# Which engine adds the squared tiles: four tiles per retention head and per state-space group, on VectorE instead of GpSimd

## The chip, the cores and the metric

The kernel runs on one core of one Trainium2 chip. The metric is the device time of one execution in microseconds; several executions are timed and their median is compared. Besides, one execution was recorded by the hardware profiler, and all rows below come from it. PE is TensorE (PEld its weight loads), DVE is VectorE, ACT is ScalarE, POOL is GpSimd and SP is SyncE, which here only issues DMAs.

## The reference

The kernel computes a small network of three layers on 256 tokens of 1024 channels, in fp32. Two parts matter here.

The retention mixer has four heads. For each, `ret` (512 channels) is normalised over its own channels and multiplied with a gate:

```python
ret = (intra + cross.swapaxes(0, 1)).reshape(bsz, seq, B_HEADS, B_DV)
ret = rms_norm(ret, out_g.reshape(B_HEADS, B_DV)).reshape(bsz, seq, dv)
y = ret * jax.nn.silu(g.astype(jnp.float32))
```

The state-space mixer has four groups of 512 channels, and normalises each in the same way after the gate:

```python
y = y.reshape(b, seq, D_INNER).astype(h.dtype) * jax.nn.silu(z)
y = rmsnorm(y.reshape(b, seq, SSD_GROUPS, D_INNER // SSD_GROUPS),
            ssd_norm_w.reshape(SSD_GROUPS, D_INNER // SSD_GROUPS))
```

Each such norm needs, per token, the sum of the squares of 512 channels.

## The kernel before

Channels lie on the 128 partitions and tokens along the free axis, so 512 channels are four tiles of 128x256. All weights come from one stream of 381 slabs (128x1024 fp32, 512 KB each) through a ring of six buffers. SP loads a slab once DVE has finished with its buffer; ACT copies it, rounded, into `w_hi` (L177); DVE writes the rest into `w_lo` (L182, "the split"); PE multiplies each of eight blocks three times (L190 to L192). ACT is four slabs ahead of the one being multiplied, DVE three.

The sum of squares goes over three engines. ACT squares four tiles into `sq`. POOL adds tiles 2 and 3 onto 0 and 1 (128x512, L258), then tile 1 onto tile 0 (128x256, L260); this is `add_four`. PE multiplies `sq[:, 0]` with a matrix of ones, which adds over the partitions. DVE and ACT make the inverse root of it, DVE puts it on a diagonal (`diag`), PE spreads it, and the result scales the tiles.

The order of the work is written out by hand for each engine, as a list of steps j = 0 to 11, one per slab of a head or group; engines meet only at semaphores. Retention head h runs straight for h = 0 and as a hardware loop for the other three. On PE, `sums` (L1137) stands behind slab j = 10 and the spread of `diag` (L1163) behind slab 11. On DVE, step j = 10 is a split, then `g_b` (L1256), which waits for PE's slab 10; step 11 is a split, the norm's root (L1250 to L1253), and `g_b` again.

State-space groups likewise run once straight and three times in a loop. The norm of group g is done in the steps of group g + 1 (`tail`), that of the last group in the steps of the 16 gate slabs that follow. On DVE each step j < 6 of the loop is a split and three taps of a convolution over PE's result (L1738, after ACT's L1595 has made the first tap); step 3 begins with the norm's root (L1697 to L1700), step 6 with four products `y_f` (L1704), from which ACT makes `b_hi` (L1542). PE sums the squares behind slab 2 (`tail_sums`, L1400). Behind slab 6 it transposes tiles 2 to 5 (L1439), behind slab 8 it multiplies the first decayed head pair (L1451), which comes from ACT's exponentials (L1570) and DVE's product with the mask (L1763).

In the gates, DVE also computes the pooled windows (`pool`: L1789 to L1795, `pooled_lo`: L1800).

POOL's queue holds, besides the additions, loads of the modulation weights (L390, six per retention head; the last one stands behind that head's `add_four`), the store of the cumulative sums and one broadcast of them per group (L2150), and two small stores of 1024 single elements each (L2155, L2156), which stand behind the `add_four` of the last group.

Of the kernel before, what the change touches and what calls it, by code (L numbers as in the profile page):

```python
# [10 lines left out]
ALU = mybir.AluOpType  # L11
# [56 lines left out]
def val(base, it=None, step=0):  # L68

    return base if it is None else it * step + base  # L70
# [21 lines left out]
def build(nc, x, stream, ada, c_rows, params, consts, out):  # L92
    ctx = ExitStack()
    with ctx:
# [157 lines left out]
            pool.wait_ge(sq_added, ADDED[v] - NT + m)  # L252
            pool.tensor_tensor(sq[:, 0], sq[:, 0], sq[:, m], ALU.add).then_inc(sq_added, 1)

        def add_four(pool, done, base):

            pool.wait_ge(done[0], done[1])
            pool.tensor_tensor(sq[:, 0:2], sq[:, 0:2], sq[:, 2:4], ALU.add).then_inc(sq_added, 1)  # L258
            pool.wait_ge(sq_added, base + 1)
            pool.tensor_tensor(sq[:, 0], sq[:, 0], sq[:, 1], ALU.add).then_inc(sq_added, 1)  # L260

        def ready(s, base):

# [128 lines left out]
        def first_block_pool(pool):  # L392

            pool.wait_ge(o_lo_ready, HEADS_A)
            pool.dma_start(cond_row, c_rows).then_inc(cond_in, 16)
            for i in range(2):
                ada_load(pool, i)
            add_pairs(pool, 1)
            for i in range(2, FFN_DOTS + 3):
                ada_load(pool, i)  # L400
            add_pairs(pool, 2)
            out_b = FFN_DOTS + HEAD_DOTS * HEADS_B
            for h in range(HEADS_B):
                first = FFN_DOTS + HEAD_DOTS * h
                for i in range(first + 3, first + 2 + HEAD_DOTS):
                    ada_load(pool, i)
                add_four(pool, (ret_sq, 2 * h + 2), ADDED_RET + 2 * h)
                ada_load(pool, first + 2 + HEAD_DOTS)
            loads = {m: out_b + 3 + m for m in range(5)}
            loads.update({6: out_b + 8, 7: out_b + 9})  # L410
            for m in range(NT):
                if m in loads:
                    ada_load(pool, loads[m])
                if m:
                    add_tile(pool, 3, m)
            for i in range(out_b + 10, ADA_TILES):
                ada_load(pool, i)
# [793 lines left out]
        def retention_vec(dve, step):  # L1211
# [8 lines left out]
            def head(h, it=None):  # L1220
# [9 lines left out]
                for j in range(12):  # L1230
                    s = S_B + HEAD * h + j
                    if h or j != 2:
                        split_lo(dve, s + 3, it, HEAD)
                    if h == 0 and j == 1:
                        tables()
                    if j in DOT_AT:
                        n = DOT_AT.index(j)
                        dot(dve, FFN_DOTS + HEAD_DOTS * h + n, head_dots[:, n:n + 1], it, HEAD_DOTS // 3)
                    if j == 1:
                        rotary(q_rot, 0, s + 1)  # L1240
                    if j == 3:
                        dve.wait_ge(rot_ready, per_head(1, 2, h, it))
                        rotary(k_rot, 2, s + 1)
                    if j == 7:
                        dve.wait_ge(qk_ready, per_head(1, 1, h, it))
                        dve.tensor_tensor(decayed, ps[:, 7, 0:SEEN], const("decay", SEEN) if it is None else con[:, bass.ds(it * SEEN + CC["decay"] + SEEN * h, SEEN)],
                                          ALU.mult).then_inc(decayed_ready, 1)
                    if j == 11:
                        dve.wait_ge(ret_sum, per_head(1, 1, h, it))
                        dve.tensor_scalar(rs_var[:, 0:NB], token_sums(7), 1.0 / 512, EPS_A, ALU.mult, ALU.add).then_inc(var_ready, 1)  # L1250
                        rsqrt(dve, step, RS_RET + h, NB, rs_root[:, 0:NB], it)
                        step(dve.tensor_scalar(diag[:, 2], ident, rs_root[:, 0:1], None, ALU.mult))
                        dve.tensor_scalar(diag[:, 3], ident, rs_root[:, 1:2], None, ALU.mult).then_inc(ret_diag, 1)  # L1253
                    if j >= 8:
                        dve.wait_ge(w_used, val(s + 1, it, HEAD))
                        dve.tensor_tensor(g_b[:, j - 8], ps[:, j - 8, 0:SEQ], inv[:, :], ALU.mult).then_inc(g_taken, 1)  # L1256
# [391 lines left out]
        def ssd_vec(dve, step):  # L1648
# [39 lines left out]
            def tail(j, g, it):  # L1688

                if j == 0:  # L1690
                    skip(2, g, it)
                    skip(3, g, it)
                    dve.wait_ge(z_silu, in_group(1, 1, g, it))
                    dve.tensor_tensor(z_s, cv[:, 2:6], z_s, ALU.mult).then_inc(yz_ready, 1)
                if j == 3:
                    dve.wait_ge(ysum_ready, in_group(1, 1, g, it))
                    dve.tensor_scalar(rs_var[:, 0:NB], token_sums(5), 1.0 / 512, EPS_B, ALU.mult, ALU.add).then_inc(var_ready, 1)  # L1697
# [443 lines left out]
        def _(pool):  # L2141
# [4 lines left out]
            for g in range(GROUPS):  # L2146
# [1 line left out]
                    pool.wait_ge(first_gaps, 4 * g)  # L2148
                    pool.wait_ge(gap_ready, 12 * g)
                pool.dma_start(cum_all, cum_rows[g:g + 1].rearrange("a (h t) -> a h t", t=SEQ).broadcast_to((P, GROUP_HEADS, SEQ))).then_inc(rows_landed, 16)  # L2150
                if g:
                    add_four(pool, (ysq_ready, g), ADDED_SSD + 2 * g - 2)
            add_four(pool, (ysq_ready, GROUPS), ADDED_SSD + 2 * GROUPS - 2)
            pool.wait_ge(mod_ready, 1)
            pool.dma_start(row_cols[0].rearrange("(m p) -> p m", p=P), mod[:, 5 * NT:6 * NT], allow_slow_non_contiguous=True).then_inc(rows_stored, 16)  # L2155
            pool.dma_start(row_cols[1].rearrange("(m p) -> p m", p=P), pcol("final_w", n=NT), allow_slow_non_contiguous=True).then_inc(rows_stored, 16)  # L2156
# [177 lines left out]
```

## Time and profile before

| | us |
|---|---|
| median of 3 runs | 1263.19 (1260.96 to 1263.36) |
| the profiled execution, time / span | 1263.84 / 1262.0 |
| PE busy | 1208.2 (96%) |
| DVE busy | 964.8 (76%) |
| ACT busy | 708.2 (56%) |
| POOL busy | 85.4 (7%) |
| mean granted clock of PE | 0.984 |
| DMA from issue to landing, median: a weight slab / a broadcast of the sums | 4.0 / 7.6 |

The span reaches from the first to the last instruction of the recorded execution. An engine that is busy 96% of the time is not at its peak all that time, but there is little idle time to take away. In the timelines each row has the start in us, the length in us, the engine, the line, what is written and read, and the count; in square brackets stands how long the engine was idle ahead of the row and what ended that. Instructions of one engine overlap a little: the next one starts before the one before has ended.

### The profile page before, as it was taken

How to read it: one execution, taken by the hardware profiler on the slowest of the kernel's cores; microseconds unless marked ns; L12 is line 12 of the kernel's file. 1: busy time of each engine (PE TensorE's matmuls, PEld its weight loads, DVE VectorE, ACT ScalarE, POOL GpSimd, SP SyncE). 2: the span in 40 equal slices, each digit the busy share in tenths (PEclk: the TensorE clock that was granted, in tenths of full speed). 3: DMA queues.
4: the chain of work that ended last, by engine and by line, in shares of the span. 5: the costliest groups of instructions: out<-in, count | busy, mean ns of one | idle time of the engine just before them, and what ended most of it. 6: DMA issues, size and time to landing. Idle time of an engine off the chain costs nothing.

```text
span 1262.0 us, 25971 instructions
## 1 busy us (share of the span) xinstructions
PE 1208.2 (96%) x9260; PEld 1157.1 (92%) x9260; DVE 964.8 (76%) x1764; ACT 708.2 (56%) x1104; POOL 85.4 (7%) x104
## 2 busy tenths in 40 slices
PE   8989899999899999999999989999999999999996
PEld 7978899999899999999999978898898999899995
DVE  5766788888787897788888878988896557666665
ACT  5555655556454555465555657767775335645443
POOL 0002000000211111200000000011010002000001
PEclk9989899999999999999999989999999999999998
DMA  8334466666466866756565616455446455555550
GB/s 307 108 109 160 147 199 220 205 227 205 149 235 248 290 217 230 262 167 218 199 215 183 200 57 229 151 183 172 160 137 206 160 183 184 188 192 182 187 166 34
DMA packets 72462, 235.69 MB, mean 187 GB/s; under 512 B 7360, under 2 KB 15808, under 8 KB 72272
## 3 DMA queue, kind: packets, MB, share of 16 engines
q1 hardware_dynamic: 63728, 203.86, 48.1%
q0 software_dynamic: 8528, 30.98, 7.6%
q8 instruction: 40, 0.66, 0.2%
q14 instruction: 22, 0.18, 0.0%
q10 hardware_dynamic: 144, 0.02, 0.0%
HBM read 233.73 MB, written 1.09 MB: 186 GB/s over the span
## 4 chain that ended last, share of the span: by engine, by line
PE 71%; DVE 16%; issue 6%; ACT 5%; POOL 1%; DVEq 1%; DMA 0%; ACTq 0%; SPq 0%; PEldq 0%
PE ps L190 22%; PE ps L192 22%; PE ps L191 22%; DVE w_lo L182 6%; DVE arena L1738 2%; DVE arena L1009 1%; ACT w_hi L177 1%; DVE arena L1011 1%; DVE arena L1003 1%; ACT arena L952 1%; PE ps L1451 1%; POOL sq L243 0%; DMA w_raw<-stream 0%; ACT a_hi L317 0%; DVE b_lo L1032 0%
## 5 line engine op out<-in xcount | busy, mean ns | idle before, releaser
L190 PE MATMUL ps<-a_hi,w_hi 128*128 128x256 f32 x1656 | 479.6, 290 | 7.4 <-DVE a_lo L1320 2.6
L182 DVE TENSOR_TENSOR w_lo<-w_raw,w_hi 128x1024 fp32r<-128x1024 f32 x381 | 463.9, 1224 | 17.8 <-ACT w_hi L177 13.8
L191 PE MATMUL ps<-a_lo,w_hi 128*128 128x256 f32 x1656 | 470.6, 284 | 0.0
L192 PE MATMUL ps<-a_hi,w_lo 128*128 128x256 f32 x1656 | 470.4, 284 | 0.0
L177 ACT ACTIVATE w_hi<-w_raw 128x1024 fp32r<-128x1024 f32 x381 | 391.0, 1048 | 25.2 <-PE ps L192 21.2
L190 PEld LDWEIGHTS ps<-a_hi,w_hi 128*128 128x128 f32 x1656 | 319.3, 193 | 16.8 <-issue 9.1
L191 PEld LDWEIGHTS ps<-a_lo,w_hi 128*128 128x128 f32 x1656 | 319.8, 193 | 0.5 <-issue 0.2
L192 PEld LDWEIGHTS ps<-a_hi,w_lo 128*128 128x128 f32 x1656 | 319.6, 193 | 0.0
L190 PE MATMUL ps<-b_hi,w_hi 128*128 128x256 f32 x672 | 193.5, 288 | 9.0 <-issue 5.7
L191 PE MATMUL ps<-b_lo,w_hi 128*128 128x256 f32 x672 | 191.5, 285 | 0.0
L192 PE MATMUL ps<-b_hi,w_lo 128*128 128x256 f32 x672 | 191.5, 285 | 0.0
L190 PEld LDWEIGHTS ps<-b_hi,w_hi 128*128 128x128 f32 x672 | 130.5, 194 | 11.6 <-issue 7.3
L191 PEld LDWEIGHTS ps<-b_lo,w_hi 128*128 128x128 f32 x672 | 130.5, 194 | 0.0
L192 PEld LDWEIGHTS ps<-b_hi,w_lo 128*128 128x128 f32 x672 | 130.4, 194 | 0.0
L952 ACT ACTIVATE arena<-arena,par 128x256 f32<-128x256 f32 x88 | 53.0, 602 | 93.5 <-DVE arena L1003 93.1
L190 PE MATMUL ps<-c_hi,w_hi 128*128 128x258 f32 (+1 forms) x336 | 96.3, 286 | 2.0 <-DVE c_lo L1800 2.0
L191 PE MATMUL ps<-c_lo,w_hi 128*128 128x258 f32 (+1 forms) x336 | 95.8, 285 | 0.0
L192 PE MATMUL ps<-c_hi,w_lo 128*128 128x258 f32 (+1 forms) x336 | 95.8, 285 | 0.0
L1009 DVE SCALAR_TENSOR_TENSOR arena<-arena,par 128x255 f32<-128x255 f32 x88 | 42.3, 481 | 37.6 <-ACT arena L952 37.6
L190 PEld LDWEIGHTS ps<-c_hi,w_hi 128*128 128x128 f32 x336 | 64.5, 192 | 3.3 <-DVE c_lo L1800 2.2
L191 PEld LDWEIGHTS ps<-c_lo,w_hi 128*128 128x128 f32 x336 | 64.5, 192 | 1.1
L192 PEld LDWEIGHTS ps<-c_hi,w_lo 128*128 128x128 f32 x336 | 64.0, 191 | 0.0
(290 smaller groups left out, 1470.9 us busy)
## 6 DMA issues: line engine op xcount, KB each, us to landing
w_raw<-stream SPq DMA_DIRECT2D x381, 512.0 KB, 4.0
arena<-ada POOLq DMA_DIRECT2D x48, 512.0 KB, 4.9
c_hi<-cum_rows POOLq DMA_DIRECT2D x4, 1024.0 KB, 7.6
con<-consts SPq DMA_DIRECT2D x1, 1440.0 KB, 11.3
arena<-x SPq DMA_DIRECT2D x2, 512.0 KB, 4.4
arena<-row_cols POOLq DMA_DIRECT2D x2, 512.0 KB, 5.0
out<-arena SPq DMA_DIRECT2D x4, 256.0 KB, 2.4
arena<-c_rows POOLq DMA_DIRECT2D x1, 512.0 KB, 4.0
```

Of the source, the lines that this page charges most:

```text
L177: act.activation(w_hi[:, s % RING], w_raw[:, s % RING], ACT.Copy).then_inc(w_hi_ready, 1)
L182: dve.tensor_tensor(w_lo[:, s % RING], w_raw[:, s % RING], w_hi[:, s % RING].bitcast(F32), ALU.subtract).then_inc(w_lo_ready, 1)
L190: pe.matmul(o, wh, xh, start=start, stop=False, skip_group_check=shared)
L191: pe.matmul(o, wh, xl, start=False, stop=False, skip_group_check=shared)
L192: return pe.matmul(o, wl, xh, start=False, stop=stop, skip_group_check=shared)
L952: act.activation(conv[:, p % 2, half], up[:, p % 2, half], ACT.Identity, bias=prm(p, 6 + half, it), scale=prm(p, 3 * half + 2, it)).then_i ...
L1003: dve.tensor_tensor(up[:, p % 2, half], ps[:, 6 - 2 * (p % 2) + half, 0:SEQ], inv[:, :], ALU.mult).then_inc(f["up_out"], 1)
L1009: step(dve.scalar_tensor_tensor(out=t[:, 1:SEQ], in0=u[:, 0:SEQ - 1], scalar=prm(p, 3 * half + 1, it), in1=t[:, 1:SEQ], op0=ALU.mult, op1= ...
L1011: dve.scalar_tensor_tensor(out=t[:, 2:SEQ], in0=u[:, 0:SEQ - 2], scalar=prm(p, 3 * half, it), in1=t[:, 2:SEQ], op0=ALU.mult, op1=ALU.add). ...
L1451: pe.matmul(o[i], x_tok2[:, 0, j * SSD_P:(j + 1) * SSD_P], seen[j % 4][:, 0:SEQ], start=True, stop=False)
L1738: ins = dve.scalar_tensor_tensor(out=cv[:, j, n:SEQ], in0=ps[:, j % 4, 0:SEQ - n], scalar=prm(5 * j + 3 - n, g, it), in1=cv[:, j, n:SEQ], ...
```

## The change

`add_four` now runs on DVE, with the same two additions. In the retention heads it stands in step 10, between the split and `g_b`, behind a wait for ACT's squares. In the groups it stands at the head of step 2, ahead of the split; in the gates also at the head of step 2, behind the first pooled windows. The order of all other steps is unchanged, and POOL goes from one DMA to the next.

```diff
-        def add_four(pool, done, base):
-
-            pool.wait_ge(done[0], done[1])
-            pool.tensor_tensor(sq[:, 0:2], sq[:, 0:2], sq[:, 2:4], ALU.add).then_inc(sq_added, 1)
-            pool.wait_ge(sq_added, base + 1)
-            pool.tensor_tensor(sq[:, 0], sq[:, 0], sq[:, 1], ALU.add).then_inc(sq_added, 1)
+        def add_four(dve, n, per, it):
+
+            for i, width in enumerate((2, 1)):
+                dve.wait_ge(sq_added, val(n + i, it, per))
+                dve.tensor_tensor(sq[:, 0:width].rearrange("p m t -> p (m t)"), sq[:, 0:width].rearrange("p m t -> p (m t)"),
+                                  sq[:, width:2 * width].rearrange("p m t -> p (m t)"), ALU.add).then_inc(sq_added, 1)
...
                 for i in range(first + 3, first + 2 + HEAD_DOTS):
                     ada_load(pool, i)
-                add_four(pool, (ret_sq, 2 * h + 2), ADDED_RET + 2 * h)
                 ada_load(pool, first + 2 + HEAD_DOTS)
...
+                    if j == 10:
+                        dve.wait_ge(ret_sq, per_head(2, 2, h, it))
+                        add_four(dve, ADDED_RET + 2 * h, 2, it)
                     if j == 11:
...
+                if j == 2:
+                    dve.wait_ge(ysq_ready, in_group(1, 1, g, it))
+                    add_four(dve, ADDED_SSD + 2 * g, 2, it)
                 if j == 3:
...
-                if g:
-                    add_four(pool, (ysq_ready, g), ADDED_SSD + 2 * g - 2)
-            add_four(pool, (ysq_ready, GROUPS), ADDED_SSD + 2 * GROUPS - 2)
             pool.wait_ge(mod_ready, 1)
```

Behind the change most line numbers are 2 to 5 higher or lower. On DVE, in the loop over groups, the end of step 1 and the begin of step 2 read so before (an ISA or REGISTER_ALU row only prepares or waits; L1738 are the taps, L182 is the split):

```order
L1738 SCALAR_TENSOR_TENSOR arena<-ps,par,arena 128x253
L181 REGISTER_ALU
L182 TENSOR_TENSOR w_lo<-w_raw,w_hi 128x1024 [waits w_hi_ready]
L1736 REGISTER_ALU
L1738 ISA [waits tap_done]
```

and now (the taps are L1743, the additions L259):

```order
L1743 SCALAR_TENSOR_TENSOR arena<-ps,par,arena 128x253
L258 ISA [waits ysq_ready]
L259 TENSOR_TENSOR sq<-sq 128x512 [waits sq_added]
L258 REGISTER_ALU
L259 TENSOR_TENSOR sq<-sq 128x256 [waits sq_added]
L181 REGISTER_ALU
L182 TENSOR_TENSOR w_lo<-w_raw,w_hi 128x1024 [waits w_hi_ready]
L1741 REGISTER_ALU
L1743 ISA [waits tap_done]
```

Two operations came in between the last tap of step 1 and the split of step 2; nothing was taken out. On DVE, in the loop over retention heads, steps 9 to 11 read so before (L1256 is `g_b`):

```order
L1256 TENSOR_TENSOR arena<-ps,inv 128x256 [waits w_used]
L181 REGISTER_ALU
L182 TENSOR_TENSOR w_lo<-w_raw,w_hi 128x1024 [waits w_hi_ready]
L1256 TENSOR_TENSOR arena<-ps,inv 128x256 [waits w_used]
L181 REGISTER_ALU
L182 TENSOR_TENSOR w_lo<-w_raw,w_hi 128x1024 [waits w_hi_ready]
L1250 TENSOR_SCALAR rs_var<-ps 128x2 [waits ret_sum]
```

and now (`g_b` is L1258):

```order
L1258 TENSOR_TENSOR arena<-ps,inv 128x256 [waits w_used]
L181 REGISTER_ALU
L182 TENSOR_TENSOR w_lo<-w_raw,w_hi 128x1024 [waits w_hi_ready]
L1248 REGISTER_ALU
L258 REGISTER_ALU [waits ret_sq]
L259 TENSOR_TENSOR sq<-sq 128x512 [waits sq_added]
L258 REGISTER_ALU
L259 TENSOR_TENSOR sq<-sq 128x256 [waits sq_added]
L1258 TENSOR_TENSOR arena<-ps,inv 128x256 [waits w_used]
```

The additions stand behind the split of step 10 and ahead of the `g_b` that waits for PE's slab 10. On POOL, from the store of the cumulative sums on, the queue was and is (+):

```order
-L2144 DMA cum_rows<-arena 32x256 [waits dt_ready]
-L2150 DMA c_hi<-cum_rows 128x8x256 [waits rows_stored]
-L2150 DMA c_hi<-cum_rows 128x8x256 [waits gap_ready,first_gaps]
-L258 TENSOR_TENSOR sq<-sq 128x512 [waits ysq_ready]
-L260 TENSOR_TENSOR sq<-sq 128x256 [waits sq_added]
...
-L2155 DMA row_cols<-mod 128x8x1 [waits mod_ready]
-L2156 DMA row_cols<-par 128x8x1
+L2149 DMA cum_rows<-arena 32x256 [waits dt_ready]
+L2155 DMA c_hi<-cum_rows 128x8x256 [waits rows_stored]
+L2155 DMA c_hi<-cum_rows 128x8x256 [waits gap_ready,first_gaps] x3
+L2157 DMA row_cols<-mod 128x8x1 [waits mod_ready]
+L2158 DMA row_cols<-par 128x8x1
```

The two small stores stand directly behind the last broadcast now.

## Rows read from the trace of the kernel before

**Rows 1.** POOL's two additions: count, ns min/median/max, first and last start in us.

```profile
L258 POOL TENSOR_TENSOR sq<-sq x8: 1287/1299/1816, 354.1 to 920.3; 128x512 f32<-128x512 f32 x8
L260 POOL TENSOR_TENSOR sq<-sq x8: 738/744/1627, 355.5 to 922.1; 128x256 f32<-128x256 f32 x8
```

**Rows 2.** Timeline of DVE in a retention head: two dependent additions and the next split.

```profile
378.93 0.42 DVE L1227 TENSOR_TENSOR arena<-arena 128x256 f32<-128x256 f32 x1
379.38 0.43 DVE L1228 TENSOR_TENSOR arena<-arena 128x256 f32<-128x256 f32 x1
379.73 1.22 DVE L182 TENSOR_TENSOR w_lo<-w_raw,w_hi 128x1024 fp32r<-128x1024 f32 x1
```

**Rows 3.** Timeline of DVE, step 10 of a retention head.

```profile
435.26 1.22 DVE L182 TENSOR_TENSOR w_lo<-w_raw,w_hi 128x1024 fp32r<-128x1024 f32 x1
437.80 0.42 DVE L1256 TENSOR_TENSOR arena<-ps,inv 128x256 f32<-128x256 f32 x1 [1.32 <-PE ps L192]
```

**Rows 4.** Timeline of PE's weight loads in the same head: sum and spread.

```profile
437.49 0.53 PEld L1137 LDWEIGHTS ps<-con,sq 128*128 128x128 f32 x4
...
441.15 0.30 PEld L1163 LDWEIGHTS ps<-diag,con 128*128 128x128 f32 x2 [0.27 <-DVE diag L1253]
```

**Rows 5.** Timeline of DVE in the second turn of the group loop.

```profile
830.43 1.23 DVE L1694 TENSOR_TENSOR arena<-arena 128x1024 f32<-128x1024 f32 x1 [0.87 <-ACT arena L1529]
...
837.13 1.22 DVE L182 TENSOR_TENSOR w_lo<-w_raw,w_hi 128x1024 fp32r<-128x1024 f32 x1
...
848.34 1.73 DVE L1738 SCALAR_TENSOR_TENSOR arena<-ps,par,arena 128x255 f32<-128x255 f32 x3
...
850.45 1.66 DVE L1704 SCALAR_TENSOR_TENSOR arena<-arena,par 128x256 f32<-128x256 f32 x4
```

**Rows 6.** Timeline of PE's weight loads in the first and second turn.

```profile
815.80 0.20 PEld L1451 LDWEIGHTS ps<-arena 128*64 128x64 f32 x4 [1.79 <-issue]
...
836.80 0.53 PEld L1400 LDWEIGHTS ps<-con,sq 128*128 128x128 f32 x4
...
850.57 0.53 PEld L1439 LDWEIGHTS ps<-con,arena 128*128 128x128 f32 x5 [0.67 <-ACT arena L1554]
...
858.92 0.20 PEld L1451 LDWEIGHTS ps<-arena 128*64 128x64 f32 x4 [1.71 <-issue]
```

**Rows 7.** Timeline of ACT in the second turn.

```profile
847.41 0.56 ACT L1595 ACTIVATE arena<-ps,par 128x256 f32<-128x256 f32 x1 [1.05 <-PE ps L192]
...
852.25 1.06 ACT L1542 ACTIVATE b_hi<-arena 128x1024 f32 x1 [1.73 <-DVE arena L1704]
```

**Rows 8.** Timeline of DVE in the gates.

```profile
920.91 1.24 DVE L1793 TENSOR_TENSOR arena<-arena,con 128x16 f32<-128x16 f32 x2
922.18 1.22 DVE L1795 SCALAR_TENSOR_TENSOR arena<-arena 128x512 f32<-128x512 f32 x1
...
930.98 0.26 DVE L1793 TENSOR_TENSOR arena<-arena,con 128x16 f32<-128x16 f32 x2
931.27 0.69 DVE L1795 SCALAR_TENSOR_TENSOR arena<-arena 128x512 f32<-128x512 f32 x1
...
933.91 0.69 DVE L1800 TENSOR_TENSOR c_lo<-arena,c_hi 128x512 fp32r<-128x512 f32 x1 [0.68 <-ACT c_hi L1630]
```

**Rows 9.** Timeline of PE's weight loads in the gates: the sum.

```profile
923.04 0.53 PEld L1400 LDWEIGHTS ps<-con,sq 128*128 128x128 f32 x4
```

**Rows 10.** The last broadcast, and weight loads issued 872 to 880, then 922 to 926.

```profile
865.36 0.90 POOL L2150 DMA_DIRECT2D c_hi<-cum_rows  x1 [29.19 <-DVE arena L1725]
...
L2085 SPq DMA_DIRECT2D w_raw<-stream x2: 332/332/333, 876.1 to 878.9; - x2
...
DMA to landing us min/median/max: 3.4/3.4/3.4
...
DMA to landing us min/median/max: 12.8/12.8/12.8
```

**Rows 11.** Timeline of ACT: it takes up the slab loaded at 876.1.

```profile
888.42 1.05 ACT L177 ACTIVATE w_hi<-w_raw 128x1024 fp32r<-128x1024 f32 x1
```

## Prediction

> **What bounds the kernel now.** I read the page's engine totals first (the table above): PE is busy for 96% of the span, DVE for 76%, POOL for 7%. POOL is idle nearly all the time, so what the change takes off it is worth nothing by itself; the question is where DVE has room. The second view is the list of the two lines that do the adding [rows 1]: eight pairs, four in the retention stage (from 354 us) and four in the state-space stage (to 922 us). Third come the timelines of DVE, PE and ACT around the places where the pairs will stand. The reader is to see three different situations there.
>
> In a retention head DVE waits for PE. Behind the split of slab j = 10 it stands idle for 1.32 us until the next use of a PE result [rows 3]. PE runs without a stop except 0.27 us at the end of the head, where it waits for `diag` [rows 4].
>
> In the loop over state-space groups it is the reverse. From 830.43 to 852.1 DVE goes from one instruction straight to the next (but for some 0.3 us in which ACT takes a root): product with z, then splits and taps of six tiles, then the norm's products [rows 5]. ACT waits for the last of them (1.73 us), turns it into `b_hi`, goes on to the exponentials, DVE multiplies these with the mask, and PE stands at L1451 for 1.71 us until that is done [rows 6, 7]. The next turn begins with that PE work, so this is a closed circle: whatever lengthens DVE's run lengthens every turn. PE's own waits in a turn are 0.67 us (L1439) and 1.71 us (L1451) [rows 6].
>
> In the gates after the last group PE is ahead until the sixth slab: DVE waits 0.68 us for ACT's `c_hi`, which waits for that slab [rows 8].
>
> **The change part by part.** Removed from POOL: 8 pairs of 1.30 and 0.74 us [rows 1]. Nobody waits for POOL in the trace at either place: the squares are summed by PE at 437.49 and at 836.80, without an idle time before it [rows 4, 6]. Gain 0.
>
> Added to DVE: 8 pairs. A 128x512 operation with both inputs in SBUF has a row of 0.69 us on DVE, a 128x256 addition rows of 0.42 and 0.43; a dependent one starts 0.03 us after the end of the one before, and an independent one 0.35 us after its predecessor's start [rows 2, 8]. So a pair holds DVE for 0.69 + 0.03 + 0.35 = 1.07 us, and its result is there after 0.69 + 0.03 + 0.42 = 1.14 us. In the group loop three taps of 0.48 us take 1.73 [rows 5], 0.15 us between dependent instructions, but they have register-held addresses and the additions have none; with that gap the pair would be 1.19 us. I take 1.07 and keep 1.19 as the upper end. DVE's new wait for the squares is nothing: in program order ACT makes them at least a slab ahead, and at the tightest place, the last, POOL had them at 920.3 [rows 1] and DVE comes for them at 921.9 (below).
>
> Retention heads, x4. The split begins at 435.26 and the pair can start 1.14 us later, at 436.40; the result is there at 437.54, DVE is free at 437.47, and before the change it was idle until 437.80 [rows 3]. DVE's order behind it does not move: the next split, the norm (L1250) and `diag` come when they came. PE wanted the sum at 437.49 and gets it at about 437.58: 0.1 us. PE stood 0.27 us at the head's end anyway [rows 4], so this is absorbed. Term 0, at most 4 x 0.1. If the cover were gone (a pair of 1.5 us), each head would pay the excess over 1.4. One load of the modulation weights per head stood behind the pair on POOL's queue and is now issued some 2 us earlier; it is used only in the next head.
>
> Group loop, turns 1 to 3, x3. The pair stands ahead of the split at 837.13. DVE's run is longer by 1.07. PE wants the squares' sum at 836.80, but DVE comes to the pair only at 837.13 and has it at 838.27: PE, which did not wait here, now waits 1.5 us, with slabs 3 to 5 queued behind. This is not added to the 1.07: PE's next wait, 0.67 us at L1439, is for a tile that comes from DVE over ACT and moves with DVE, so PE's lateness beyond DVE's own (0.3 to 0.45 us) falls into it. One thing follows from it: the ACT operation of tile 5 waits for PE's slab (1.05 us idle before 847.41, 0.56 long) [rows 7]. With PE 1.5 later it ends at 849.5, and DVE would want it at 848.34 + 1.07 = 849.41. So DVE loses about 0.12 more there: 1.07 + 0.12 = 1.2 us a turn, 3.6 us for three. Both ends: 1.07 a turn (3.2) if tile 5 is in time, 1.19 + 0.12 (3.9) with the longer gap, 1.52 (4.6) if PE's wait came through in full, and 0 if something other than DVE sets the turn.
>
> Gates, x1. POOL's pair ran against DVE here. Two DVE operations with both inputs in SBUF took 1.24 and 1.22 us where the same ones took 0.26 and 0.69 ten microseconds later [rows 8]: 1.51 us lost to POOL. The page "SBUF — State Buffer" of the Trainium skill (Who interferes with whom) says that a DVE instruction with two SBUF inputs and a GpSimd one that reads SBUF exclude each other for a whole instruction; by that rule, the trace agrees. With POOL silent DVE reaches the pair at 921.9 (920.91 + 0.29 + 0.73) and finishes it at 923.07, where PE wants it at 923.04 [rows 9]: some 0.1 us later. DVE is then 0.4 us earlier than before, but meets the wait for the sixth slab (0.68 us) [rows 8], so this brings nothing. The term is +0.1, between 0 and +0.3.
>
> In the loop it was POOL that waited: its 0.74 us addition stretched to as much as 1.63 us [rows 1], while DVE ran on, so nothing is given back there.
>
> Moved on POOL's queue: the two small stores of gate and gain rows (L2155, L2156) stood behind the last pair, so after 922.1 [rows 1]. They now follow the last broadcast, at about 867 [rows 10]. After them, before, a weight load took 12.8 us to land instead of 3.4 [rows 10]. ACT asks for the slab loaded at 876.1 only at 888.42, 12.3 us later [rows 10, 11]. If the stores begin only when the broadcast has landed (865.4 + 7.6, the median in the table, = 873) and block the loads for the 9.4 us more that were seen and some spare, to 883.5, that slab lands near 887.5: in time. Term 0, between 0 and +2.
>
> Sum: 0 + 3.6 + 0.1 + 0 = +3.7 us. The profiled execution took 1263.84 us (span 1262.0 and 1.8 around it); with the change 1267.5. It lies 0.65 above the median of 1263.19, so I predict a median of 1266.9.
>
> **The rivals.** (a) The circle is not DVE's. If the turn is set by ACT with its table loads and DVE's run has slack that the rows hide, the pairs vanish into waits in all eight places, and the gates give back 0.4 us: 1263.19 - 0.4 = 1262.8, not slower. Its place is PE's wait at L1451; it decides if that wait shrinks while the turn stays at 858.92 - 815.80 = 43.1 us [rows 6]. For it: PE has 0.67 + 1.71 us of waits a turn to spend. Against it: DVE has next to no idle time from 830.43 to 852.1, and ACT waits 1.73 us for DVE's last product [rows 5, 7].
>
> The page "Perfetto Trace Analysis" of the skill (Optimizing Scalar/DVE Operations) holds that moving work between GpSimd and DVE might not help, as they share a port; that speaks of the overlap, which in the loop costs DVE nothing here, so the trace bears the rule out only in the gates.
>
> (b) The early stores starve the stream in the last turn. For it: the 12.8 us landing. Against it: the ring's 12.3 us of lead. If a slab comes 1 to 4 us late while ACT and DVE are in the circle, the time is 1266.9 + 1 to 4, about 1269.5.
>
> (c) PE's new wait of 1.5 us comes through in full, because what its later waits are for moves as far: 3 x 1.52 + 4 x 0.1 + 0.1 = 5.1, or 1263.19 + 5.1 = 1268.3. For it: ACT takes five results of PE's late slabs in the turn. Against it: four of these reads are behind other work of ACT's that moves by 1.07 only.
>
> **How the numbers follow.** Forecast (1266.3 to 1267.8) 0.66; (a) 0.14; (b) 0.09; (c) 0.08; something unseen on the fast side 0.03. The three runs shown spread over 2.4 us, so the median itself may be off by one. What a measurement can tell from no change is 0.2%, 2.5 us, that is 1265.7. Forecast, (b) and (c) lie above it, with 0.83; about 0.07 of that is lost to the spread, and 0.76 is left. Same: (a) and what falls back, 0.20. Faster 0.04. The range of 8 in 10 leaves out most of (a) and the far end of (b): 1263.9 to 1270.0.
>
> **What would show it.** In the changed profile POOL has 16 additions fewer, and DVE 16 more of about 0.69 and 0.42 us. In the loop the turn (distance between broadcasts on POOL's queue) goes from 43.1 to about 44.3 us, PE waits about 1.5 us before the squares' sum, PE's wait at L1439 shrinks to about 0.3 us and that at L1451 stays at 1.7. In the retention heads PE's last wait goes from 0.27 to about 0.2 us, and their length stays. In the gates the two stretched operations are 0.26 and 0.69 again. The weight load near 925 lands in 4 us, and the slow landing stands near 876. The prediction is wrong if the turn stays at 43.1, or if it grows by over 1.6 us.

## The result, and the profile after

| | before | after |
|---|---|---|
| median, us (8 runs each) | 1263.15 (1260.79 to 1264.19) | 1265.65 (1265.05 to 1267.66) |
| ratio of times, 95% interval | | 1.0028 (1.0017 to 1.0038) |
| profiled execution, time / span | 1263.84 / 1262.0 | 1265.14 / 1263.4 |
| busy PE / DVE / POOL | 1208.2 / 964.8 / 85.4 | 1206.6 / 972.0 / 64.9 |
| mean granted clock | 0.984 | 0.987 |

Of 1263.15 us the ratio is 3.5 us, with an interval of 2.1 to 4.8. The change makes the kernel slower. Forecast were +3.7 us and a median of 1266.9. The measured median lies 1.25 us below that, under the narrow forecast (1266.3 to 1267.8) and inside the range of 1263.9 to 1270.0; the two medians differ by only 2.5 us, in times that spread over 3.4 us before and 2.6 us after.

**The spans can't be subtracted.** Those of the two profiled executions differ by only 1.4 us. Ahead of the changed work are two stretches in which PE was granted different clocks. The windows read: stretch, its length, busy time and count of PE, PEld, DVE, ACT and POOL, the clock, the DMA share, GB/s. Before:

```profile
76.00:88.00 12.00, 11.42 (x68) 10.78 (x68) 7.73 (x25) 7.50 (x20) 0.00 (x0) 0.72 0.40 129
330.00:343.00 13.00, 13.00 (x72) 11.63 (x72) 10.57 (x20) 5.46 (x6) 0.57 (x1) 0.92 0.34 121
```

After (the second stretch begins 2.7 us earlier, so that it ends with the same work):

```profile
76.00:88.00 12.00, 11.42 (x78) 10.46 (x77) 8.35 (x25) 8.29 (x20) 0.00 (x0) 0.83 0.43 132
327.30:340.30 13.00, 13.00 (x80) 11.64 (x79) 11.90 (x26) 5.47 (x6) 0.57 (x1) 1.00 0.36 122
```

At 0.72 the trace has 68 matmuls in 12 us, at 0.83 it has 78; at 0.92 and 1.00 it is 72 and 80 in 13 us. The begin of the second stretch, taken finer (before, then after, where the same work comes 1.2 us earlier):

```profile
328.00:332.00 4.00, 4.00 (x23) 4.00 (x22) 2.51 (x8) 0.20 (x1) 0.00 (x0) 0.57 0.02 4
326.80:330.80 4.00, 4.00 (x34) 3.95 (x34) 2.79 (x9) 0.90 (x3) 0.00 (x0) 1.00 0.01 4
```

Before, PE spent most of these 4 us at the lower of its two clock levels (1.2 instead of 2.4 GHz): its weight loads stood 0.21 us apart, and 0.12 us apart ahead of that. In both executions PE had stood idle for 2.27 us ahead of L234. From its sum at L234 to its spread at L273 it took 4.80 us before (327.26 to 332.06) and 3.30 after (326.06 to 329.36). That is 1.5 us. The first stretch gives 1.0: ACT copies the same slabs at 65.37 and 65.34 us ahead of it, at 92.44 and 91.38 behind it. At the begin of the retention stage the changed kernel's execution is 2.7 us ahead, though no instruction up to there differs; 2.5 of it lie in these two stretches. Other kernels of this study had 0.74 and 0.78 in the first stretch, 0.95 and 0.98 in the second. So I compare distances between equal instructions from there on:

| stretch, us | before | after | difference |
|---|---|---|---|
| retention, PE's first to last load of `diag` (L1163 before, L1162 after) | 117.86 | 118.01 | +0.15 |
| from there to the first decayed pair (L1451 before, L1453 after) | 292.20 | 292.40 | +0.20 |
| first turn of the loop (from one first decayed pair to the next) | 43.18 | 44.28 | +1.10 |
| second turn | 43.12 | 44.43 | +1.31 |
| third turn | 43.13 | 44.43 | +1.30 |
| gates, to PE's wait for DVE's `c_lo` | 50.04 | 50.02 | -0.02 |

The sum is 4.0 us, of which 3.7 lie in the three turns, and 4.0 is within the ratio's 2.1 to 4.8.

**The loop.** PE's weight loads of the changed kernel, with L1402 for L1400 in [rows 6], L1441 for L1439 and L1453 for L1451:

```profile
814.56 0.20 PEld L1453 LDWEIGHTS ps<-arena 128*64 128x64 f32 x4 [1.72 <-issue]
...
837.09 0.52 PEld L1402 LDWEIGHTS ps<-con,sq 128*128 128x128 f32 x4 [1.46 <-DVE sq L259]
...
850.63 0.86 PEld L1441 LDWEIGHTS ps<-con,arena 128*128 128x128 f32 x8 [0.46 <-ACT arena L1556]
...
858.99 0.20 PEld L1453 LDWEIGHTS ps<-arena 128*64 128x64 f32 x4 [1.72 <-issue]
...
903.42 0.20 PEld L1453 LDWEIGHTS ps<-arena 128*64 128x64 f32 x4 [1.73 <-issue]
```

There is a new wait of 1.46 us for the squares, but the turn is longer by only 1.3: 0.2 us came out of the wait at L1441 (0.67 before), and that at the first decayed pair is unchanged (1.72, 1.71 before). DVE, which answers to [rows 5]:

```profile
835.90 1.14 DVE L259 TENSOR_TENSOR sq<-sq 128x512 f32<-128x512 f32 x2
836.96 1.22 DVE L182 TENSOR_TENSOR w_lo<-w_raw,w_hi 128x1024 fp32r<-128x1024 f32 x1
...
847.04 1.22 DVE L182 TENSOR_TENSOR w_lo<-w_raw,w_hi 128x1024 fp32r<-128x1024 f32 x1
848.39 1.74 DVE L1743 SCALAR_TENSOR_TENSOR arena<-ps,par,arena 128x255 f32<-128x255 f32 x3
```

The pair takes 1.14 us and the split starts 1.06 us after it. The taps of tile 5 start 1.35 us after their split; elsewhere it is 1.13 (838.09 behind 836.96). These 0.22 us are the second part of the turn's 1.3. They come from ACT, which got PE's slab late ([rows 7] had an idle time of 1.05 here):

```profile
847.69 0.56 ACT L1597 ACTIVATE arena<-ps,par 128x256 f32<-128x256 f32 x1 [1.51 <-PE ps L192]
```

**The retention heads and the gates.** DVE in step 10 of the head of [rows 3]:

```profile
432.65 1.22 DVE L182 TENSOR_TENSOR w_lo<-w_raw,w_hi 128x1024 fp32r<-128x1024 f32 x1
433.78 1.15 DVE L259 TENSOR_TENSOR sq<-sq 128x512 f32<-128x512 f32 x2
435.18 0.42 DVE L1258 TENSOR_TENSOR arena<-ps,inv 128x256 f32<-128x256 f32 x1 [0.26 <-PE ps L192]
```

The pair fills the former 1.32 us of idle time down to 0.26, and `g_b` starts 2.53 us after the split's start, as before (2.54). PE's last wait in the head is 0.17 us:

```profile
438.53 0.30 PEld L1162 LDWEIGHTS ps<-diag,con 128*128 128x128 f32 x2 [0.17 <-DVE diag L1255]
```

In the gates the two stretched operations of [rows 8] are 0.26 and 0.69 again, and the pair follows:

```profile
922.29 0.26 DVE L1798 TENSOR_TENSOR arena<-arena,con 128x16 f32<-128x16 f32 x2
922.59 0.69 DVE L1800 SCALAR_TENSOR_TENSOR arena<-arena 128x512 f32<-128x512 f32 x1
923.32 1.15 DVE L259 TENSOR_TENSOR sq<-sq 128x512 f32<-128x512 f32 x2
```

**The moved stores.** POOL's queue, and the weight load that was issued at 876.1, which before landed in 3.4 us [rows 10]:

```profile
865.42 0.88 POOL L2155 DMA_DIRECT2D c_hi<-cum_rows  x1 [43.55 <-DVE arena L1730]
866.29 0.90 POOL L2157 DMA_DIRECT2D row_cols<-mod  x1
867.18 0.88 POOL L2158 DMA_DIRECT2D row_cols<-par  x1
```

```profile
L2090 SPq DMA_DIRECT2D w_raw<-stream x1: 333/333/333, 876.1 to 876.1; - x1
...
DMA to landing us min/median/max: 7.6/7.6/7.6
```

The loads of 922 to 930 now land in 3.5 to 4.1 us, instead of 12.8. The slow landing has moved along with the stores. The load directly behind them, issued at 868.3, has no landing in this trace, so 7.6 us is not the longest; the run e4_early_stores has it. ACT takes the slab of 876.1 up 13.4 us after its load was issued (889.55), so no one waits for it.

### The profile page after: what moved, and what is told of

It is laid out like the page before. It is cut to its first block, busy times and chain, and to the rows that moved or that the text cites. A ratio compares the mean times of both kernels' runs of the same rounds, so it can differ in the third digit from the quotient of the medians.

```text
span 1263.4 us, 25987 instructions
## 1 busy us (share of the span) xinstructions
PE 1206.6 (96%) x9260; PEld 1154.1 (91%) x9260; DVE 972.0 (77%) x1780; ACT 708.1 (56%) x1104; POOL 64.9 (5%) x88
## 4 chain that ended last, share of the span: by engine, by line
PE 63%; DVE 21%; issue 7%; ACT 6%; DVEq 1%; POOL 1%; DMA 0%; ACTq 0%; SPq 0%; PEldq 0%
PE ps L190 19%; PE ps L192 19%; PE ps L191 19%; DVE w_lo L182 8%; DVE arena L1008 2%; DVE arena L1002 2%; DVE arena L1010 2%; ACT arena L951 1%; DVE arena L1743 1%; DVE b_lo L1031 1%; ACT w_hi L177 1%; PE ps L1453 1%; POOL sq L243 0%; DVE arena L1709 0%; DMA w_raw<-stream 0%
## 5 line engine op out<-in xcount | busy, mean ns | idle before, releaser
L182 DVE TENSOR_TENSOR w_lo<-w_raw,w_hi 128x1024 fp32r<-128x1024 f32 x381 | 464.2, 1225 | 17.5 <-ACT w_hi L177 13.8
```

Source lines behind the costliest of these rows:

```text
L182: dve.tensor_tensor(w_lo[:, s % RING], w_raw[:, s % RING], w_hi[:, s % RING].bitcast(F32), ALU.subtract).then_inc(w_lo_ready, 1)
```

## The experiments

Two theories went into them. A: DVE's run closes the circle of the loop, so the pair costs its own length there and nothing elsewhere. C (rival c): PE's new wait of 1.5 us costs in full, since what PE waits for later moves as far. Rivals a (something else closes the circle) and b (the early stores) are tried with them. Every ratio is against the kernel before on the same chip.

**Retention alone (e1_retention_only).** The change in the heads; in the groups and the gates POOL adds as before.

```diff
-                if j == 2:
-                    dve.wait_ge(ysq_ready, in_group(1, 1, g, it))
-                    add_four(dve, ADDED_SSD + 2 * g, 2, it)
...
+                if g:
+                    add_four_pool(pool, (ysq_ready, g), ADDED_SSD + 2 * g - 2)
```

> Only the four retention pairs are on VectorE; the state-space pairs stay on GpSimd, and so do the small stores behind them. My theory (the cost is all in the group loop): no change, ratio 1.000, at most +0.4 us; the group turn stays at 43.1 us, PE's wait at the end of a head is 0.17 to 0.19 us as with the whole change. If the retention pairs carried a part of the measured +3.5 us, this kernel would be over 1 us slower and its heads longer than 39.3 us.

Measured: 1262.13 against 1263.23, ratio 0.9997 (0.9988 to 1.0006). PE's wait at a head's end is 0.18 us. No time of a whole run can tell this from no change. The distances can: from PE's first load of `diag` to its last it is 118.00 us here, and from there to the first decayed pair 292.41. In all five kernels with this pair on DVE (the change, this one, e3_pair_in_step_1, e12_change_in_new_order and, for the second distance, e5_retention_doubled) these are 118.00 to 118.01 and 292.31 to 292.43; in the eight with it on POOL 117.81 to 117.87 and 292.19 to 292.27. So the four retention pairs cost about 0.3 us together, a tenth of what the groups cost.

**Groups alone (e2_groups_only).** The opposite: POOL adds in the heads, DVE in the groups and the gates.

```diff
-                    if j == 10:
-                        dve.wait_ge(ret_sq, per_head(2, 2, h, it))
-                        add_four(dve, ADDED_RET + 2 * h, 2, it)
...
+                add_four_pool(pool, (ret_sq, 2 * h + 2), ADDED_RET + 2 * h)
```

> Only the four state-space pairs are on VectorE; the retention pairs stay on GpSimd. My theory: the whole cost, +3.6 to +3.7 us (ratio 1.0029), turns of 44.4 us and the small stores behind the last broadcast as in the whole change. If the two halves shared the cost, about +1.8.

Measured: 1266.77, ratio 1.0025 (1.0015 to 1.0035). The turns are 44.30, 44.45 and 44.44 us, with PE's wait of 1.46 at the sum. Nearly the whole loss is in the groups.

**The pair one step earlier (e3_pair_in_step_1).** In the looped turns the pair stands ahead of the split of step 1, 3 us earlier, so PE has its sum in time, while DVE does the same work.

```diff
-                if j == 2:
+                if j == (2 if it is None else 1):
```

> The whole change, but in the three looped turns the pair stands at the head of step 1 on VectorE, ahead of its split, not of step 2. The squares are ready there (ACT ends them at 833.1, VectorE comes at 834.4), and the sum is there before PE asks for it. Theory A (VectorE's length sets the turn, PE's wait for the sum adds only the small extra at tile 5): the 1.4 us wait at the sum goes, PE's wait at the transposes grows from 0.45 to about 1.7 us, and a turn costs 1.07 instead of 1.25 to 1.3 over before, so the kernel is some 0.6 us faster than the whole change and still 3.2 us slower than before. Rival (c) (PE's wait for the sum is what lengthens the turn): the turn falls back to about 43.1 us and the time to that of before.

Measured: 1266.48, ratio 1.0028 (1.0017 to 1.0040). DVE's pair, then PE's weight loads:

```profile
834.87 1.14 DVE L259 TENSOR_TENSOR sq<-sq 128x512 f32<-128x512 f32 x2
```

```profile
837.31 0.53 PEld L1402 LDWEIGHTS ps<-con,sq 128*128 128x128 f32 x4
...
852.15 0.85 PEld L1441 LDWEIGHTS ps<-con,arena 128*128 128x128 f32 x8 [1.74 <-ACT arena L1556]
...
860.51 0.20 PEld L1453 LDWEIGHTS ps<-arena 128*64 128x64 f32 x4 [1.72 <-issue]
...
904.70 0.20 PEld L1453 LDWEIGHTS ps<-arena 128*64 128x64 f32 x4 [1.72 <-issue]
```

PE does not wait at the sum; the same time stands at L1441 instead, which had 0.67 before and has 1.74 now, 1.07 more. The turn is 904.70 - 860.51 = 44.19 us, 1.06 over the one before and 0.24 under that of the change. With the wait of 1.46 us taken away, 1.06 of the 1.30 stay: this is what DVE's length costs, as A has it. The other 0.24 go with PE's wait, so C is wrong in its size, but not in every part. The three turns together are 0.6 us shorter than in the change; the medians (1266.48 and 1265.65) don't resolve it, only the turns do.

**The stores early, without the rest (e4_early_stores).** The kernel before, with both small stores behind the last broadcast.

```diff
+                if g == GROUPS - 1:
+                    pool.wait_ge(mod_ready, 1)
+                    pool.dma_start(row_cols[0]..., mod[:, 5 * NT:6 * NT], ...)
+                    pool.dma_start(row_cols[1]..., pcol("final_w", n=NT), ...)
                 if g:
                     add_four(pool, (ysq_ready, g), ADDED_SSD + 2 * g - 2)
```

> The kernel before, with all additions on GpSimd, but with the two small stores directly behind the last broadcast. Theory A: no change (0 within 0.5 us); the slow weight loads move from around 925 to around 870 us, and no engine waits for one. Rival (b): a slab comes late in the last turn, that turn is 1 us or more longer than the two before it.

Measured: 1263.56, ratio 1.0001 (0.9992 to 1.0010). The weight load directly behind the stores, issued at 868.3, landed in 12.9 us (6.0 before, beside the broadcast), those of 876.2 to 879.0 in 5.9 to 7.4 us, that of 924.9 in 3.5. ACT takes up the slab of 868.3 only at 886.56, 5.4 us after it has landed, and nobody waits for a DMA. Rival b falls.

**The retention pair doubled (e5_retention_doubled).** Over the change, two more additions of the same sizes, into tiles that nobody reads, behind each retention pair.

```diff
                         add_four(dve, ADDED_RET + 2 * h, 2, it)
+                        dve.tensor_tensor(sq[:, 4:6]..., sq[:, 2:4]..., sq[:, 2:4]..., ALU.add)
+                        dve.tensor_tensor(sq[:, 6], sq[:, 3], sq[:, 3], ALU.add)
```

> The whole change, with a second pair of additions of the same sizes behind each retention pair (into tiles 4 to 6 of sq, which nobody reads). It costs VectorE about 0.95 us more per head. Theory A: the cover in a head is the 1.32 us that VectorE waited; 0.26 us of it is left beside the pair, so 0.6 to 0.7 us per head come out at the other side: norm and diag later, PE's wait at the head's end 0.8 instead of 0.17 us, heads 0.6 us longer, +2.5 us over the whole change (1268). If a head has more cover than that row shows, PE's wait stays below 0.4 and the time at the whole change's.

Measured: 1269.14 against 1263.36, ratio 1.0043 (1.0027 to 1.0058). Timeline of DVE and PE's last wait of the head:

```profile
436.91 1.15 DVE L259 TENSOR_TENSOR sq<-sq 128x512 f32<-128x512 f32 x2
437.97 0.68 DVE L1251 TENSOR_TENSOR sq<-sq 128x512 f32<-128x512 f32 x1
...
438.91 0.42 DVE L1261 TENSOR_TENSOR arena<-ps,inv 128x256 f32<-128x256 f32 x1
...
442.25 0.30 PEld L1162 LDWEIGHTS ps<-diag,con 128*128 128x128 f32 x2 [0.77 <-DVE diag L1258]
```

DVE has no idle time ahead of `g_b` any more, PE waits 0.77 instead of 0.17 us, and the heads take 39.75 to 39.91 instead of 39.33, some 2 us for four if the first grew like the others. The cover in a head is thus nearly used up by one pair: 0.26 us of it are left on DVE, and what exceeds it reaches PE.

**PE late, DVE free, by way of POOL (e7_sum_late_on_pool).** The kernel before; in the looped turns POOL makes two idle additions ahead of the pair, so that the sum comes as late as in the change.

```diff
                 if g:
+                    for i in range(2):
+                        pool.tensor_tensor(sq[:, 4:6], sq[:, 2:4], sq[:, 2:4], ALU.add)...
                     add_four(pool, (ysq_ready, g), ADDED_SSD + 2 * g - 2)
```

> The kernel before, with two more 128x512 additions on GpSimd ahead of the pair in each looped group turn (into tiles 4 and 5 of sq, which nobody reads). VectorE does nothing more; only the sum comes late, so PE waits for it, by my estimate 1.5 to 2.5 us. It measures the price of PE's lateness alone. Theory A: the first 0.4 us of PE's wait is free, since the first tap of tile 5 has that much lead on VectorE, and the rest comes through to the turn: turn = 43.1 + (wait - 0.4). With a wait of 1.5 that is +1.1 a turn, which is as long as VectorE's pair made it: two separate limits, of which the change pays the longer. Rival: PE has 2.4 us of waits in a turn and hides all of it, turn 43.1 to 43.3.

Measured: 1268.23, ratio 1.0044 (1.0032 to 1.0056); turns of 45.57, 44.54 and 44.51 us. It doesn't isolate PE's lateness, because DVE was not free:

```profile
836.34 2.05 DVE L183 TENSOR_TENSOR w_lo<-w_raw,w_hi 128x1024 fp32r<-128x1024 f32 x1
...
839.95 1.47 DVE L183 TENSOR_TENSOR w_lo<-w_raw,w_hi 128x1024 fp32r<-128x1024 f32 x1
```

```profile
835.16 2.15 POOL L2155 TENSOR_TENSOR sq<-sq 128x512 f32<-128x512 f32 x2 [10.06 <-ACT sq L1533]
837.39 2.15 POOL L259 TENSOR_TENSOR sq<-sq 128x512 f32<-128x512 f32 x1
```

The splits take 2.05 and 1.47 us instead of 1.22, and POOL's first addition of the pair 2.15 instead of 1.30. DVE lost 1.08 to POOL, and some 0.3 more at tile 5, where its taps start 1.43 instead of 1.13 us behind their split. The expectation that DVE does nothing more was wrong. How late PE was can still be read:

```profile
817.77 0.20 PEld L1452 LDWEIGHTS ps<-arena 128*64 128x64 f32 x4 [1.80 <-issue]
...
840.39 0.52 PEld L1401 LDWEIGHTS ps<-con,sq 128*128 128x128 f32 x4 [1.54 <-POOL sq L261]
```

From the first decayed pair to the sum it took 22.62 us instead of 21.00, 1.62 more, and in the first turn 2.59 more. The next run shows what such lateness costs.

**PE late alone (e11_pe_late_alone).** A cleaner form: in the looped turns of the kernel before, PE makes its loads and products for the sum four times over (16 loads instead of 4), so that it is nearly as late as in the change. DVE and POOL are left alone.

```diff
-                for b in range(NB):
+                for b in range(NB) if it is None else [b for _ in range(4) for b in range(NB)]:
```

> The kernel before, but PE makes the sum of squares four times over instead of once in the looped group turns (same operands, same result; six more matmuls). PE is later by about 3 x 0.45 = 1.35 us behind slab 2, VectorE does nothing more and GpSimd nothing else than before: this is PE's lateness by itself, which the run with the late sum on GpSimd did not give, since GpSimd's additions shut VectorE out there for 1.1 us. Theory A: 0.4 us of it is free (the lead of tile 5's first tap on VectorE), so the turn is 43.1 + 1.35 - 0.4 = 44.1 us and VectorE shows an idle time of about 0.9 us at tile 5 and none elsewhere. Rival: PE's 2.4 us of waits in the turn swallow it, turn 43.1 to 43.2.

Measured: 1266.39 against 1263.43, ratio 1.0025 (1.0016 to 1.0034). PE's weight loads, then DVE:

```profile
836.80 1.87 PEld L1400 LDWEIGHTS ps<-con,sq 128*128 128x128 f32 x16
...
860.05 0.20 PEld L1451 LDWEIGHTS ps<-arena 128*64 128x64 f32 x4 [1.72 <-issue]
...
904.31 0.20 PEld L1451 LDWEIGHTS ps<-arena 128*64 128x64 f32 x4 [1.73 <-issue]
```

```profile
849.46 0.48 DVE L1738 SCALAR_TENSOR_TENSOR arena<-ps,par,arena 128x255 f32<-128x255 f32 x1 [0.83 <-ACT arena L1595]
```

PE is late by 1.87 - 0.53 = 1.34 us and the turn is 44.26, 1.13 longer. DVE gains new idle time at tile 5, 0.83 us for ACT, and some 0.2 at tile 4 just before. So there is a second circle just beside DVE's: slab, ACT's first tap, DVE's taps, with 1.34 - 1.13 = 0.21 us of room.

In the change both come late together, and the turn pays the larger of the two, not their sum. DVE's length is worth 1.06 (e3_pair_in_step_1). PE's lateness from the first decayed pair to the sum is 837.09 - 814.56 = 22.53 us instead of 836.80 - 815.80 = 21.00, so 1.53, and less the room 1.32; the turn grew by 1.31. The same working gives 1.41 for the second turn of e7_sum_late_on_pool, where 44.54 - 43.12 = 1.42 was measured, and 2.38 for its first, where it was 45.57 - 43.18 = 2.39. So it is PE's lateness, by way of ACT's first tap, that sets the changed turn, and DVE's length stands 0.26 us behind it. Both come from the pair's place in DVE's run.

**DVE relieved (e8_pool_splits_one).** The opposite sign: in the kernel before POOL also makes one split of each looped turn.

```diff
+                    pool.wait_ge(w_lo_ready, s6)
+                    split_lo(pool, s6)
...
-                    if j < 7:
+                    if j < 7 and not (g and j == 3):
                         split_lo(dve, S_GRP + GRP * g + j + 3, it, GRP)
```

> The kernel before, with the opposite move: in the looped turns GpSimd also makes one of VectorE's weight splits (step 3, 128x1024), behind its pair. VectorE's run is 1.14 us shorter. Theory A with the tile 5 limit: VectorE gains 0.37 us a turn and then waits for ACT and PE at tile 5, so the turn is 42.8 and the kernel 1.1 us faster than before. If VectorE's length alone set the turn, 42.0 us and 3.4 us faster. If GpSimd's longer operation shuts VectorE out of its operations with two SBUF inputs, no gain or a loss.

Measured: 1262.68, ratio 0.9995 (0.9985 to 1.0004). The turn is 900.33 - 857.42 = 42.91 us, only 0.22 shorter, less than expected (0.37), though 1.14 us of work went off DVE:

```profile
837.14 2.41 POOL L182 TENSOR_TENSOR w_lo<-w_raw,w_hi 128x1024 fp32r<-128x1024 f32 x1 [2.25 <-DVE w_lo L182]
```

```profile
843.69 1.74 DVE L1740 SCALAR_TENSOR_TENSOR arena<-ps,par,arena 128x255 f32<-128x255 f32 x3 [0.24 <-ACT arena L1595]
846.83 1.74 DVE L1740 SCALAR_TENSOR_TENSOR arena<-ps,par,arena 128x255 f32<-128x255 f32 x3 [0.28 <-ACT arena L1595]
```

DVE runs into the same second circle at tiles 4 and 5. The room beside DVE's run is 0.2 us, from this side too.

**ACT's wait filled (e9_gaps_in_the_wait).** In the circle ACT waits 1.73 us for DVE's last product and then makes the gaps and the exponentials, while DVE's mask waits. Here ACT makes the gaps of the first two heads within that wait, and DVE masks them one step earlier. The additions stay on POOL.

```diff
                     if j == 6:
                         silu(5)
+                        act.wait_ge(rows_landed, in_group(16, 16, g, it))
+                        if not g:
+                            act.wait_ge(own_copied, 1)
+                        gaps(0)
+                        gaps(1)
...
                     if j == 7:
+                        mask(0)
+                        mask(1)
                         gaps(2)
                         gaps(3)
```

> The kernel before, with another order in the same circle: ACT makes its first four gap tiles (1.48 us) in the 1.73 us in which it waits for VectorE's norm products, not after b_hi, and VectorE masks heads 0 and 1 before its own gaps of heads 2 and 3. Theory A (the turn is the chain VectorE, ACT, VectorE, PE up to L1451): the exponentials start 1.4 us earlier, VectorE reaches the mask 1.1 us earlier, PE's wait at L1451 goes from 1.7 to about 0.6 us, each turn is 1.1 us shorter, and with the straight first group the kernel is 3.3 to 4 us faster than before, 0.3%. If PE or the weights set the turn, it stays at 43.1 and PE waits elsewhere.

Measured: 1260.32, ratio 0.9972 (0.9960 to 0.9984), faster than the kernel before and than the changed one. ACT, then PE:

```profile
848.62 1.48 ACT L1562 ACTIVATE arena<-c_hi,arena 128x256 f32<-128x256 f32 x4
850.44 1.06 ACT L1542 ACTIVATE b_hi<-arena 128x1024 f32 x1 [0.34 <-DVE arena L1702]
```

```profile
855.98 0.20 PEld L1451 LDWEIGHTS ps<-arena 128*64 128x64 f32 x4 [0.57 <-issue]
...
897.96 0.20 PEld L1451 LDWEIGHTS ps<-arena 128*64 128x64 f32 x4 [0.57 <-issue]
```

The gaps' 1.48 us have gone into the wait, PE stands 0.57 instead of 1.71 us at the first decayed pair, and the turn is 41.98 us, 1.15 shorter.

**Both (e10_gaps_and_split).** The last two edits together.

> Both edits that made the kernel before shorter: ACT's gap tiles in its wait with the mask of heads 0 and 1 pulled ahead, and one VectorE split per looped turn on GpSimd. Theory A: the second is held to the 0.2 us that tile 5 allows, and the two add up: turn 41.8 us, time 4.1 us below before (0.9968). If VectorE's length alone set the turn in the new order, another 1.1 us per turn.

Measured: 1258.76, ratio 0.9967 (0.9955 to 0.9979), turn 897.34 - 855.57 = 41.77 us. It is the fastest version of the study, about 4 us below the kernel before; the split brings the same 0.21 us a turn as alone, which the ratios can't tell from nothing.

**The change in the new order (e12_change_in_new_order).** The whole change with the edit of e9_gaps_in_the_wait.

> The whole change (pairs on VectorE) together with the new order of gaps and masks. Theory A: VectorE still runs without a pause in the turn, so the pair costs what it cost before, 1.25 to 1.3 us a turn; the turn is 43.3 us and the kernel is within 0.4 us of the kernel before. If the new order had opened room on VectorE, the turn would stay near 42.0.

Measured: 1261.82, ratio 0.9996 (0.9987 to 1.0006). PE:

```profile
858.46 0.20 PEld L1453 LDWEIGHTS ps<-arena 128*64 128x64 f32 x4 [0.57 <-issue]
...
901.72 0.20 PEld L1453 LDWEIGHTS ps<-arena 128*64 128x64 f32 x4 [0.57 <-issue]
```

The turn is 43.26 us, 1.28 over the 41.98 of the new order with POOL. With PE's wait at the first decayed pair down to a third, the pair costs the same: its price doesn't hang on that wait.

## Why the prediction was right, step by step

- **The retention term, 0.** Right within its "at most 4 x 0.1". The pair lies in DVE's idle time for PE's slab [rows 3]; e1_retention_only had 0.9997 (0.9988 to 1.0006). By the distances it is 0.3 us and not 0: half of it within the heads, half on the way from there to the group loop. My limit of 1.4 us was about right too: the doubled pair takes 438.91 - 436.91 = 2.0 us, 0.6 beyond it, and a head grew by 0.4 to 0.6 in e5_retention_doubled.
- **The loop term, 3 x 1.2.** Right in its mechanism, and slightly small: 3.7 us in the three turns, 1.10, 1.31 and 1.30, for a forecast of 3.6. The 1.07 for the pair agrees with e3_pair_in_step_1 (1.06). The term for tile 5 was mis-sized: 0.12 forecast, though its own figures (849.5 and 849.41) make it 0.09, and 0.22 in the timeline, 0.24 in the turn. I had let DVE start when ACT's first tap ends, at 849.5 on the clock of before; I left out that 0.14 us passes between the end of ACT's operation and the start of DVE's. In the changed kernel ACT ends at 847.69 + 0.56 = 848.25 and DVE starts at 848.39.
- **PE's wait at the sum is not added.** Right: 1.46 us (1.5 forecast) with L1439's successor at 0.46 (about 0.3 forecast) and the decayed pair at 1.72 (1.7). Rival c would have had 1.52 a turn. Its working had a true core, though, that my text took for a small extra at one operation: PE's lateness costs all but 0.21 us of itself with DVE's length unchanged (e11_pe_late_alone), and in the change it is this limit, 1.32, that ends last, not DVE's 1.06. That 1.2 came near 1.3 is because the prediction added to DVE's length what PE's path has beyond it, which is the same as taking the larger.
- **The gates, +0.1.** The step was right and its end was not. Counted from the last first-pair load (L1451 at 902.05 before, L1453 at 903.42 after), the pair was to start at 921.9 - 902.05 = 19.85 us and started at 923.32 - 903.42 = 19.90; PE took the sum (L1402 at 924.52) at 21.10 us instead of 20.99: the 0.1 us. It was given back later, in a wait that I had not looked at. This is PE's weight load in the changed kernel; before, the same row stands at 952.09 with a wait of 2.20:

```profile
953.44 0.19 PEld L190 LDWEIGHTS ps<-c_hi,w_hi 128*128 128x128 f32 x1 [2.08 <-DVE c_lo L1805]
```

- **The moved stores, 0.** Right: e4_early_stores had 1.0001 (0.9992 to 1.0010). The slab of 876.1 landed sooner than my working had it (11.4 us there, 7.6 seen). The load held up most is that of 868.3, with 12.9 us in e4_early_stores, and my text did not look at it.
- **The base.** The sum was made on a profiled execution of 1263.84, and it gave 1267.5 there. The profiled execution of the changed kernel took 1265.14, 2.4 less. It had a lead of 2.7 us, most of it by the clock, and the 0.3 the other way are what the work itself cost beyond the sum. That +3.7 stands so near the ratio's 3.5 is partly luck: the distances say 4.0, with 0.3 in the retention pairs, where I had 0, and nothing left of the gates' 0.1, and the ratio's interval is 2.7 us wide.
- **Rival a** falls with e2_groups_only and e3_pair_in_step_1: the turn grew by the pair's length. What speaks for it, that PE had 2.4 us of waits a turn, is no evidence of room: both waits are ends of the same circle.

What remains open: the 0.15 us in the retention stage and the 0.2 behind it come with the retention pairs (e1_retention_only), but by which instruction is not shown. The first turn grew by 1.10 only, where PE's lateness (22.39 - 21.00 = 1.39) less 0.21 asks for 1.18. In e3_pair_in_step_1 it also grew by less than the others, 0.94 instead of 1.07. The cause of this was not found.

## What to carry to other kernels

Find the engine that has no idle rows in the closed circle of a stage: work moved onto it costs its whole length in every turn (1.06 us here for a pair of 1.07), and more if another engine gets its result late (1.31), while the same work beside a wait for PE cost less than 0.1 us here. Look for a second circle close behind the first: with 0.2 us of room between them, relieving the one brings no more than that (e8_pool_splits_one). Taking work off an engine that is idle 93% of the time, and for which nobody waits, brings nothing. The gain was in another place: an engine (here ACT) that waits for the critical one, while other work of the same circle is already there to be done.

## What the runs showed of the hardware

- **GpSimd can shut VectorE out.** In the loop of the kernel before it was POOL's second addition that stretched (1.63 instead of 0.74 us, below), beside a DVE split of 1.22; with two more additions on POOL ahead of the pair DVE's splits took 2.05 and 1.47 us instead of 1.22 (e7_sum_late_on_pool). The page "SBUF — State Buffer" of the Trainium skill (Who interferes with whom) says that a DVE instruction with two SBUF inputs contends with a GpSimd one that reads SBUF; these rows agree. Two of DVE's taps, which read one of their tensors from PSUM, kept their 1.11 us beside POOL in the same turn.

```profile
834.54 1.63 POOL L260 TENSOR_TENSOR sq<-sq 128x256 f32<-128x256 f32 x1
```

- **Single-element stores hold up the weight stream.** With two stores of 1024 elements each on POOL's queue, the 512 KB load issued 1 us behind them landed in 12.8 us in the gates and in 12.9 directly behind the broadcast (e4_early_stores), where 3.4 is usual and 6.0 beside the broadcast alone. Loads issued 8 us later still took 9.5 us at the first place and 7.4 to 7.6 at the second.
- **The same instructions had other clocks.** In the stretch at 76 us the granted clock was 0.72, 0.74, 0.78 and 0.83 in four executions, and in that at 330 us 0.92 to 1.00. Between two of them this came to 2.5 of the 2.7 us by which they stood apart, about as much as the effect that was looked for.
